# Macaron conv trunk on eight cores: Square issued early, first tiles reordered, conv tail issued later

## The reference, cut to what matters

```python
def rms_norm(x, g):
    xf = x.astype(jnp.float32)
    y = xf * lax.rsqrt(jnp.mean(xf * xf, axis=-1, keepdims=True) + RMS_EPS)
    return (y * g.astype(jnp.float32)).astype(x.dtype)

def swiglu(x, w_gate, w_up, w_down):
    return (jax.nn.silu(x @ w_gate) * (x @ w_up)) @ w_down

def conformer_conv_mixer(x, buf, w_pw1, b_pw1, w_dw, b_dw, ln_g, ln_b, w_pw2, b_pw2):
    h = x @ w_pw1 + b_pw1
    a, g = jnp.split(h, 2, axis=-1)
    v = a * jax.nn.sigmoid(g)
    c, new_buf = causal_dwconv(v, buf, w_dw)          # width 31
    c = jax.nn.silu(layer_norm(c + b_dw, ln_g, ln_b))
    return c @ w_pw2 + b_pw2, new_buf

def short_gated_conv_mixer(x, buf, w_in, w_conv, w_out):
    b_gate, c_gate, h = jnp.split(x @ w_in, 3, axis=-1)
    c, new_buf = causal_dwconv(c_gate * h, buf, w_conv)  # width 3
    return (b_gate * c) @ w_out, new_buf
```

## Time and profile before

| | us |
|---|---|
| runs of the kernel | 2915.18 and 3027.04, median 2971.11 |
| the profiled execution | 2919.62 |
| its span on the slowest core (core 3) | 2918.0 |
| spans of the eight cores | 2897.6 to 2918.0 |
| PE busy with matmuls in the span | 2644.1 (91%) |
| DVE busy | 1174.7 (40%) |
| ACT busy | 544.4 (19%) |
| mean granted TensorE clock of the cores | 0.953 to 0.957 |

### The profile page before, as it was taken

How to read it: one execution, slowest core, us unless ns; L and a number is a source line. 1 busy time by engine, 2 the same in 40 slices (tenths; PEclk the granted TensorE clock), 3 DMA queues, 4 the chain that set the end, 5 groups by cost and what they waited for, 6 DMA issues and landing times.

```text
span 2918.0 us, 37080 instructions; the slowest of 8 cores (2897.6 to 2918.0 us)
## 1 busy us (share of the span) xinstructions
PE 2644.1 (91%) x14152; PEld 1209.9 (41%) x14152; DVE 1174.7 (40%) x1737; ACT 544.4 (19%) x880; POOL 253.2 (9%) x200
## 2 busy tenths in 40 slices
PE   3999999698888779999997999999788889999995
PEld 1444444243333334444442444444333434444442
DVE  5232222635776561322226132232654462322327
ACT  3101101222233221011012101101233221011012
POOL 0000000002444000000000000000000000000000
PEclk9999999899999889999998999999899899999998
DMA  7232321232000022323212232322212222323223
GB/s 163 30 45 32 48 35 24 29 63 45 1 1 1 1 29 30 45 34 46 35 24 29 30 44 30 44 32 34 31 22 39 29 29 30 44 30 44 30 30 116
DMA packets 183643, 107.76 MB, mean 37 GB/s; under 512 B 9264, under 2 KB 175152, under 8 KB 183472
## 3 DMA queue, kind: packets, MB, share of 16 engines
q0 software_dynamic: 166464, 83.90, 22.7%
q1 hardware_dynamic: 17008, 21.50, 2.4%
HBM read 178.59 MB, written 10.68 MB: 65 GB/s over the span
## 4 chain that ended last, share of the span: by engine, by line
PE 82%; DVE 9%; DMA 4%; ACT 2%; issue 2%; SPq 0%; DVEq 0%; ACTq 0%; POOL 0%; POOLq 0%
PE ps L409 21%; PE ps L404 21%; PE ps L437 20%; PE ps L686 7%; PE ps L782 6%; DVE arena L350 3%; DVE arena L345 2%; PE ps L547 2%; PE ps L542 2%; PE ps L331 1%; PE ps L735 1%; DMA arena<-xT 1%; PE ps L882 1%; DMA arena<-b_w_in 1%; DMA arena<-ffn_w_down 1%
## 5 line engine op out<-in xcount | busy, mean ns | idle before, releaser
L404 PE MATMUL ps<-arena 128*128 128x512 bf16 (+1 forms) x3520 | 703.8, 340 | 24.5 <-DVE arena L350 23.3
L409 PE MATMUL ps<-arena 128*128 128x512 bf16 (+1 forms) x3520 | 703.1, 340 | 12.5 <-DMA arena<-ffn_w_up 12.5
L437 PE MATMUL ps<-arena 128*128 128x512 bf16 (+1 forms) x3520 | 649.1, 343 | 42.9 <-DVE arena L440 22.2
L415 DVE TENSOR_TENSOR arena<-arena,ps 128x512 bf16<-128x512 f32 (+1 forms) x440 | 248.8, 582 | 996.8 <-ACT arena L413 996.8
L413 ACT ACTIVATE arena<-ps 128x512 f32<-128x512 f32 (+1 forms) x440 | 216.9, 513 | 1490.2 <-PE ps L409 1489.5
L437 PEld LDWEIGHTS ps<-arena 128*128 128x128 bf16 x3520 | 297.0, 99 | 389.3 <-issue 70.7
L404 PEld LDWEIGHTS ps<-arena 128*128 128x128 bf16 x3520 | 301.2, 98 | 365.7 <-issue 38.6
L409 PEld LDWEIGHTS ps<-arena 128*128 128x128 bf16 x3520 | 301.1, 98 | 351.0 <-issue 23.7
L440 DVE SCALAR_TENSOR_TENSOR arena<-ps,arena 128x512 f32<-128x512 f32 (+1 forms) x480 | 276.1, 586 | 330.2 <-PE ps L437 320.1
L686 PE MATMUL ps<-arena 128*128 128x512 bf16 x992 | 229.2, 390 | 31.9 <-DVE arena L516 31.9
L782 PE MATMUL ps<-arena 128*128 128x512 bf16 (+1 forms) x960 | 183.4, 350 | 25.1 <-DMA arena<-b_w_in 17.9
(11 more groups left out here) (69 smaller groups left out, 1009.3 us busy)
## 6 DMA issues: line engine op xcount, KB each, us to landing
arena<-ffn_w_gate POOLq DMA_DIRECT2D x44, 512.0 KB, 7.6
arena<-ffn_w_up POOLq DMA_DIRECT2D x44, 512.0 KB, 5.7
arena<-ffn_w_down POOLq DMA_DIRECT2D x32, 512.0 KB, 7.4
arena<-xT SPq DMA_DIRECT2D x4, 2048.0 KB, 29.7
yT<-arena SPq DMA_DIRECT2D x4, 2048.0 KB, 6.9
arena<-ffn_w_down POOLq DMA_DIRECT2D x16, 384.0 KB, 6.3
arena<-a_w_pw POOLq DMA_DIRECT2D x12, 512.0 KB, 8.6
arena<-b_w_in POOLq DMA_DIRECT2D x12, 512.0 KB, 7.8
```

The source lines that it names most:

```text
L404: P.emit("pe", (lambda e, k=k, jj=jj, t0=t0, w=w, bg=bg, wgv=wgv: e.matmul(psum[:, bg, 0:w], wgv[:, k, jj * 128:(jj + 1) * 128], XN[:, k, ...
L409: pk = P.emit("pe", (lambda e, k=k, jj=jj, t0=t0, w=w, bu=bu, wuv=wuv: e.matmul(psum[:, bu, 0:w], wuv[:, k, jj * 128:(jj + 1) * 128], XN[: ...
L415: dd = P.emit("dve", (lambda e, s=s, w=w, bu=bu, hj=hj, t0=t0: e.tensor_tensor(out=HB[:, hj, t0:t0 + w], in0=ST[:, s, 0:w], in1=psum[:, bu ...
L437: pk = P.emit("pe", (lambda e, jj=jj, mm=mm, t0=t0, w=w, b=b, wdv=wdv, n=n: e.matmul(psum[:, b, 0:w], wdv[:, jj, mm * 128:(mm + 1) * 128], ...
```

## The change

1. `part1` is split: `part1a` is the Square on ACT, `part1b` the eight matmuls. For tile 3 `part1a` is now emitted at the end of the final stage, and `part1b` and `part2` stay where `flush_deferred` runs.
2. The first pair of chunks of a stage (of every FFN, and of the conformer's pw1) takes its ten items in another order: both chunks for tiles 0 and 1, then chunk 0 for tiles 2, 3 and 4, then chunk 1 for them. The flush comes after the second item, as before.
3. In the short conv, weights are planned, taken and released in the order C, h, B.
4. The eight applies of conv tile 3 are emitted after pw2's tile 0, through a hook; a guard makes the Squares wait until MV has been read.

Lines of the diff that only follow from these (a new signature, an order of release) are left out.

```diff
     if stop_after >= 4:
         for cp in range(4):
-            W.plan(colblock(w_bin, cp * 256), [KC, 256], "binb%d" % cp)
             W.plan(colblock(w_bin, 1024 + cp * 256), [KC, 256], "binc%d" % cp)
             W.plan(colblock(w_bin, 2048 + cp * 256), [KC, 256], "binh%d" % cp)
+            W.plan(colblock(w_bin, cp * 256), [KC, 256], "binb%d" % cp)
...
-        def part1(self, ti):
+            self.sq = {}
+
+        def part1a(self, ti):
             t0, w = TILES[ti]
             a1 = P.emit("act", (lambda e, t0=t0, w=w: e.activation(out=SQ[:, :, 0:w], in_=X[:, :, t0:t0 + w], func=AF.Square)),
-                        waits=[x_tk[ti], sq_free[0]])
+                        waits=[x_tk[ti], sq_free[0], sq_guard[0]])
+            self.sq[ti] = a1
+
+        def part1b(self, ti):
+            t0, w = TILES[ti]
+            a1 = self.sq.pop(ti)
             bank = PS.stat()
             PS.wait_free(bank)
             P.wait("pe", a1)
...
+        def part1(self, ti):
+            self.part1a(ti)
+            self.part1b(ti)
...
     def flush_deferred():
         if deferred[0] is not None:
             nrm, ti = deferred[0]
             deferred[0] = None
-            nrm.part1(ti)
+            nrm.part1b(ti)
             nrm.part2(ti)
 
     FINAL_ORDER = [4, 0, 1, 2, 3]
-
-    def tiled_final_stage(emit_tile, nxt):
+    NORMAL_ORDER = [(jj, ti) for jj in range(2) for ti in range(5)]
+    FIRST_ORDER = [(0, 0), (0, 1), (1, 0), (1, 1), (0, 2), (0, 3), (0, 4), (1, 2), (1, 3), (1, 4)]
+
+    def tiled_final_stage(emit_tile, nxt, hook=None):
         prev = None
-        for ti in FINAL_ORDER:
+        for idx, ti in enumerate(FINAL_ORDER):
             emit_tile(ti)
+            if hook is not None and hook[0] == idx:
+                hook[1]()
             if nxt is not None and prev is not None:
                 nxt.part1(prev)
                 nxt.part2(prev)
             prev = ti
         if nxt is not None:
+            nxt.part1a(prev)
             deferred[0] = (nxt, prev)
...
-                for jj in range(2):
-                    hj = jp + jj
-                    for ti, (t0, w) in enumerate(TILES):
+                first = (gi == 0 and jp == 0)
+                for it_i, (jj, ti) in enumerate(FIRST_ORDER if first else NORMAL_ORDER):
+                    if True:
+                        hj = jp + jj
+                        t0, w = TILES[ti]
...
-                        if ti == 1:
+                        if it_i == 1:
                             flush_deferred()
...
-            for cc in range(2):
-                c = cp * 2 + cc
-                for ti, (t0, w) in enumerate(TILES):
+            for it_i, (cc, ti) in enumerate(FIRST_ORDER if cp == 0 else NORMAL_ORDER):
+                if True:
+                    c = cp * 2 + cc
+                    t0, w = TILES[ti]
...
-        st_last = stat_mm(pti, pc, ptks, (6, 7))
-        d3_of[pti] = chain(pti, st_last, (6, 7))
-        apply_q.extend((pti, cc) for cc in range(KC))
-        while apply_q:
-            ati, ac = apply_q.pop(0)
-            apply(ati, ac, d3_of[ati])
-        st_free[0] = cb_free.get(("alt",))
+        st_last_f = stat_mm(pti, pc, ptks, (6, 7))
+
+        P.wait("dve", sq_free[0])
+        d3_of[pti] = chain(pti, st_last_f, (6, 7))
+
+        def m2_tail():
+            apply_q.extend((pti, cc) for cc in range(KC))
+            while apply_q:
+                ati, ac = apply_q.pop(0)
+                apply(ati, ac, d3_of[ati])
+            st_free[0] = cb_free.get(("alt",))
+            sq_guard[0] = mv_free[0]
...
-        tiled_final_stage(tile_fn, nxt)
+        tiled_final_stage(tile_fn, nxt, hook=(1, m2_tail))
```

More of the change, by code:

```diff
@@ L366, in build_program @@
     deferred = [None]
+    sq_guard = [None]
     def flush_deferred():
@@ L419, in ffn @@
                         st_free[s] = dd
-                        h_tk[ti] = dd
+                        h_tk[ti] = dd if h_tk[ti] is None or dd[1] > h_tk[ti][1] else h_tk[ti]
                         last_pe = pk
-                        if ti == 1:
+                        if it_i == 1:
                             flush_deferred()
@@ L767, in mixer_b @@
         for cp in range(4):
-            ub_, wbv, ltb = W.acquire("binb%d" % cp)
             uc_, wcv, ltc = W.acquire("binc%d" % cp)
             uh_, whv, lth = W.acquire("binh%d" % cp)
+            ub_, wbv, ltb = W.acquire("binb%d" % cp)
             for cc in range(2):
@@ L860, in mixer_b @@
                         flush_deferred()
-            W.release(ub_, last_pe)
             W.release(uc_, last_pe)
             W.release(uh_, last_pe)
+            W.release(ub_, last_pe)
         out_tks.append(P.emit("sp", lambda e: e.dma_start(out=nbp.rearrange("(c p) k -> p c k", p=128), in_=UBL),
```

## The result

The changed kernel is faster: the ratio of its time to that of the kernel before is 0.9771, with a 95% interval of 0.9759 to 0.9784. Before, the median of 10 runs was 2917.67 us; times that ratio it is 2851 us, where 2856 were predicted. The profiled execution of the changed kernel took 2851.7 us. (The plain median of its 11 runs, 3090.58, is high because in six of them the cores of one die or both had a mean granted clock of 0.81 to 0.90 instead of 0.96, as in two of the ten of the kernel before; the ratio leaves these out.)

What follows compares the result with a forecast made beforehand. Inside FFN stages only TensorE's matmul count matters, so gains lie in its waits and the low clock after them: 56 + 13 - 5.7 = 63.3 us off 2919.6 gives 2856 us, range 2838 to 2885.

Steps and rivals of the forecast that it cites:

- Part 1: Four FFN and conformer boundaries: early Square and new order of the first ten tiles save 56 us together.
- left are 1.7 + 0.5: FFN2 to FFN1 boundary: a 1.7 us wait before tile 3 plus 0.5 of low clock remain, 2.2 us.
- 1 us poorer: FFN1 to conformer boundary: its norm wait was 6.8 us instead of 7.8, so it saves 1 us less.
- The bounds: Four boundaries together: saving between 52 us (clock falls every time) and 62 us (no wait left at all).
- the 16.3 us: Excess at the FFN2 to FFN1 boundary before: Square wait 4.34, slow stat 1.5, norm wait 7.76, slow tile 3 2.7.
- The short conv: Short-conv stage: early Square and new weight order save 13 us, 7.3 at the boundary and 6 in later column pairs.
- The tail: Conv tail: moving the eight applies makes two TensorE waits of one, 2.5 us more idle and 3.1 low clock, costing 5.7.
- The sum: Whole kernel: 56 + 13 - 5.7 = 63.3 us saved, giving 2856 us.
- A: Conv tail: the deferred pairs cost TensorE nothing, so the tail gains 11.2 us; 2839 us, chance 0.06.
- B: Four boundaries: the hole before tile 3 only moves, so they give 23 us in place of 56; 2889 us, chance 0.18.
- C: Long full-clock stretches: with holes gone the granted clock falls, to 0.96 costing 104 us and giving 2960; chance 0.04.

Runs made afterwards that it cites:

- e2: The kernel before with only the Square of tile 3 moved to the end of the final stage; ratio to the kernel before 0.9872.
- e3: The kernel before with only the new order of the first ten tiles; ratio to the kernel before 0.9894.
- e5: The changed kernel with one more item that does not read tile 3 put ahead of it; executed once, 2859.2 us.
- e1: The changed kernel with only the old conv tail put back; ratio to the kernel before 0.9761, 2850.8 us.
- e7: The changed kernel with the 16-token Square in its own buffer, applies strewn among sums of tiles 0 and 1, and tile 0's Square emitted mid-tile 1; ratio 0.9730.
- e9: The changed kernel with the conv tail of e7 and the sixth weight slot of e8 together; ratio 0.9548, 2787 us.
- a_again: The changed kernel itself, unaltered, run again beside other kernels; ratio 0.9779, its profiled execution 2859.43 us.
- e8: The changed kernel with a sixth weight slot, the conformer's sample states moved into the conv buffer's space; 2799.4 us in its profiled execution.

## Why the prediction was right

*The boundaries.* Part 1 was right in mechanism. Counted at the boundary alone, as in e2 and e3, the mean of the cores fell from 16.2 to 16.4 us to 1.6 at three boundaries and from 16.2 to 1.8 at the conformer's, in both executions: 14.4 to 14.8 saved at each, 58 us in all. The prediction has 14.1 three times and 13.1, which is 55.4 (it wrote 56). The step "left are 1.7 + 0.5" was 1.46 or 1.62 of waiting and no low clock. The conformer's boundary was not "1 us poorer": on the slowest core its norm wait was shorter (6.76), but the item behind its stat ran 1.0 us slow as well. That two stretches of the table agree with 14.1 to 0.2 us is luck, since the second execution has 12.9 and 14.8 for them. The bounds were added up wrongly: by the prediction's own terms they are 4 x 12.8 - 1 = 50 and 4 x 16.3 - 1 = 64, not 52 and 62; the stated range, 2838 to 2885 us, was taken from the rivals and does not hang on them. That the remaining wait is a bank's and not the norm's was argued from the L415 product of the earlier trace rows; e5 showed it. The split of the 16.3 us between the two waits came out within 0.4 us (e2, e3).

*The short conv.* 12.2 us against 13 in one execution, 10.3 in the other. All its waits came out as worked: 3.60 at the boundary, 5.89 before tile 3 (6 expected), 2.2 in the later pairs (2.4 expected).

*The tail.* The forecast said it would cost time, by a new wait of 13.7 us in the stat of tile 4. The wait is there with 13.36. The mis-sized term is the sum, 5.7 us: the trace has 3.4. The idle time grew by 7.12 + 13.36 - 18.59 = 1.9, where 2.5 were predicted. The low clock grew by 1.4, where 3.1 were: the 80 matmuls behind the first hole took 16.26 in place of 17.31, 1.0 less, and tile 1 lost 16.25 - 13.8 = 2.4. The term took the same loss behind each hole, and it took 3.1 for it from a row that holds 0.16 us of pipeline, so that 2.9 would have been right.

*The sum.* 63.3 us were predicted (62.8 in the table's parts, with 55.4 for the boundaries), 66.7 stand in the table and 62.0 in its second execution, so the sum is right within what two executions differ by. Two terms are off beyond that, each on all eight cores: the tail cost 2.3 us less than forecast, and the four boundaries gave 3 more, 2 of them the low clock of 0.5 that did not come and 1 at the conformer's. Both push the same way, and the short conv, a little under its 13, took some of it back.

*The rivals.* A fell with e1's trace. B fell with the L404 waits: no FFN boundary keeps a wait before tile 3 above 1.5 us, and the conformer's is 1.62. C did not occur in the executions compared, whose cores had mean clocks of 0.961 to 0.969; this view shows the granted clock of the profiled one inside an FFN (columns as in the earlier trace rows):

```profile
1590.00:1970.00 380.00, 380.00 (x2137) 178.02 (x2136) 98.60 (x173) 46.13 (x93) 22.59 (x26) 1.00 0.30 38
```

It is 1.00 there, as before. The rule of the Trainium skill ("TensorE: Matmul & The Clock Gate", section "Seeing it yourself") on 13/16 of full clock with three busy cores on a die does not describe this execution.

## What to carry to other kernels

When a piece of work is put off to open a hole, look for what its own engines have queued behind it: here a Square of 0.3 us on ScalarE stood behind eight deferred pairs, TensorE's stat behind the Square, and a whole tile behind the stat. Strewing the deferred work one by one among the instructions that free banks (e7) got 18.5 us out of a stretch where moving it as a block lost 3.4. And once one wait at a boundary is gone, list the others again: the weight waits that the change left alone were worth more (e9, 2787 us) than the tail.

## What was not expected of the hardware

A short wait of TensorE costs its own length or much more. Behind waits of 1.20, 1.46 and 1.62 us the next eight matmuls ran at full speed (1.89 us in their row), behind 2.56 and 2.77 they did not (3.42 for eight, 4.07 for twelve). When the wait of 1.46 grew to 2.56, as in e9, it cost 2.8 us more, not 1.1. The length alone does not decide it: in the changed kernel, at the boundary behind pw2, cores 2 and 4 waited 2.87 and 2.88 us for up weights and ran the next eight matmuls at full speed (1.89), and in e7 the 80 matmuls behind a wait of 1.70 lost 2.8 us. What decides it was not tested.

The stretches of one kernel differ between cores with no difference in the program: the stretch from pw2 to FFN2 took 501.4 to 501.6 us on four cores of the changed kernel, 504.9 on two and 507.7 or 507.8 on two. Most of these steps arise at one wait and behind it. For FFN2's first up weights TensorE waited 2.9 to 3.1 us on the four cores, 4.8 on the next two, 5.7 and 6.1 on the last two, and lost 0.2, 1.6, and 2.7 to 2.9 us to low clock behind it. The same core is not always late: core 5 waited 6.05 in this execution and 2.92 in a_again. In e8, which has no such wait, the stretch from FFN2/0 to FFN1/1 is 491.4 to 491.5 us on seven cores and 492.6 on the eighth. Why the weights come later to some cores was not examined. The slowest core is the one that drew most of these waits, so effects of 3 us, as the tail's, need the trace of a stretch on every core rather than the time of the kernel.
